# Another order of DVE and ACT instructions at the begin of nine stages of a two-block transformer kernel

## The reference, cut to what matters

```
# first block, two layers:
h = rms_norm(x, g) * (1 + sc1) + sh1 ;  x = x + g1 * mixer(h)
h = rms_norm(x, g) * (1 + sc2) + sh2 ;  x = x + g2 * conv_ffn(h)
# second block, two layers of three sublayers each:
hn = rmsnorm(x, pre_g) * (1 + scale) + shift
y  = rmsnorm(fn(hn), post_g)            # fn: swiglu, attention, swiglu
x  = x + res_w * gate * y
```

## Time and profile before

| | us |
|---|---|
| median of 3 runs | 3943.22 (3938.38 to 3943.79) |
| the profiled execution, time | 3941.97 |
| its span, first to last instruction | 3940.2 |
| PE busy | 3712.6 (94%) |
| DVE busy | 2048.6 (52%) |
| ACT busy | 1340.0 (34%) |
| mean granted TensorE clock | 0.955 |

### The profile page before, as it was taken

The page is one execution under the profiler, slowest core; times in us unless marked ns, Lnnn a source line. Parts: engine busy times, 40 slices in busy tenths (PEclk is TensorE's granted clock), DMA queues, the critical chain, the costliest instruction groups (busy, mean ns, idle before and its releaser), DMA issues.

```text
span 3940.2 us, 42183 instructions
## 1 busy us (share of the span) xinstructions
PE 3712.6 (94%) x17108; PEld 2947.2 (75%) x17108; DVE 2048.6 (52%) x3576; ACT 1340.0 (34%) x2299; POOL 127.9 (3%) x126
## 2 busy tenths in 40 slices
PE   6899999999999999979989998999899999989998
PEld 4647888757888788856678887888677777767886
DVE  7856656776766655457653345334433333354233
ACT  3553323453323322334432232223222322233222
POOL 3330000000000000001100000000000000000000
PEclk9999999989999999989989998999899999979999
DMA  6214554414555454210122222222211121112221
GB/s 243 94 44 170 203 192 177 149 34 147 199 192 197 169 196 176 86 67 23 38 75 97 96 97 70 96 96 99 71 58 59 58 67 59 54 43 81 96 97 64
DMA packets 125023, 426.58 MB, mean 108 GB/s; under 512 B 16107, under 2 KB 21099, under 8 KB 124828
## 3 DMA queue, kind: packets, MB, share of 16 engines
q1 hardware_dynamic: 124828, 423.88, 30.8%
HBM read 421.68 MB, written 2.14 MB: 108 GB/s over the span
## 4 chain that ended last, share of the span: by engine, by line
PE 84%; DVE 11%; ACT 3%; issue 1%; POOL 0%; ACTq 0%; DVEq 0%; POOLq 0%
PE ps L409 24%; PE ps L410 24%; PE ps L411 24%; PE ps L708 1%; DVE X L1597 1%; PE ps L446 1%; PE ps L755 1%; PE ps L748 1%; DVE mrow L2051 1%; DVE TT L1516 1%; PE ps L798 1%; PE ps L787 1%; DVE HL L1505 1%; PE ps L554 1%; PE ps L453 1%
## 5 line engine op out<-in xcount | busy, mean ns | idle before, releaser
L409 PE MATMUL ps<-HH,whi 128*128 128x512 f32 x3168 | 1279.2, 404 | 71.9 <-DVE HL L1505 38.9
L410 PE MATMUL ps<-HL,whi 128*128 128x512 f32 x3168 | 1258.4, 397 | 0.0
L411 PE MATMUL ps<-HH,wlo 128*128 128x512 f32 x3168 | 1256.1, 397 | 0.0
L1453 DVE TENSOR_TENSOR wlo<-wraw,whi 128x1024 fp32r<-128x1024 f32 x526 | 643.2, 1225 | 721.8 <-ACT whi L920 721.6
L920 ACT ACTIVATE whi<-wraw 128x1024 fp32r<-128x1024 f32 x548 | 575.2, 1054 | 701.4 <-PE ps L411 694.1
L409 PEld LDWEIGHTS ps<-HH,whi 128*128 128x128 f32 x3168 | 610.8, 193 | 235.5 <-issue 77.6
L410 PEld LDWEIGHTS ps<-HL,whi 128*128 128x128 f32 x3168 | 611.8, 193 | 130.8 <-issue 4.8
L411 PEld LDWEIGHTS ps<-HH,wlo 128*128 128x128 f32 x3168 | 610.1, 193 | 131.4
L1441 DVE CUSTOM_DVE_ANT_0 mraw<-mraw,CB 128x1024 f32<-128x1024 f32 x224 | 283.0, 1264 | 1.5 <-DMA mraw<-mst 1.3
L1632 DVE TENSOR_TENSOR TT<-TT,ps 128x512 f32<-128x512 f32 x116 | 79.7, 687 | 223.1 <-PE ps L411 192.4
L409 PE MATMUL ps<-PHf,whi 128*128 128x512 f32 x352 | 136.9, 389 | 0.0
(11 more groups left out here) (329 smaller groups left out, 4044.1 us busy)
## 6 DMA issues: line engine op xcount, KB each, us to landing
wraw<-wst SPq DMA_DIRECT2D x548, 512.0 KB, 3.4
mraw<-mst SPq DMA_DIRECT2D x224, 512.0 KB, 3.5
MR<-mst SPq DMA_DIRECT2D x16, 512.0 KB, 14.2
X<-xt SPq DMA_DIRECT2D x8, 256.0 KB, 5.5
BB<-bvec SPq DMA_DIRECT2D x8, 256.0 KB, 3.7
out<-X SPq DMA_DIRECT2D x8, 256.0 KB, 2.0
CB<-crow SPq DMA_DIRECT2D x2, 512.0 KB, 4.5
BB<-bvec SPq DMA_DIRECT2D x8, 128.0 KB, 3.5
```

What stands on the lines that cost most here:

```text
L409: e.matmul(o[key], wh, sh(k), start=k == 0, stop=False)
L410: e.matmul(o[key], wh, sl(k), start=False, stop=False)
L411: ins = e.matmul(o[key], wl, sh(k), start=False, stop=k == nk - 1)
L1453: e.tensor_tensor(wlo[:, x % SPLIT, :], wraw[:, x % RAW, :], whi[:, x % SPLIT, :].bitcast(F32), ALU.subtract).then_inc(*wlo_made.up(x))
```

## The change

In `modulate` of DVE, begins E to I update one tile ahead instead of two, and low(m) comes in the same turn as b(m): update(0), b(0), update(1), low(0), b(1), update(2), low(1), and so on. The wait for the root p stands just ahead of b(0), behind update(0). In all nine begins DVE and ACT do a `feed(8)` in the turns m = 1, 4 and 6, for one block each; in E to I that is behind low(m), in A to D behind low(m-1). The first feed of each stage is shorter by these 24 tiles. Nothing is computed otherwise. The diff, with context cut:

```
@@ ACT modulate
                     e.activation(HH[:, m, :], T[m % 5], ACT.Identity, bias=MOD[:, v, m:m + 1]).then_inc(
                         *a_norm.up(("hh", s, m)))
+                    if m in (1, 4, 6):
+                        feed(8)
@@ ACT and DVE, ffn, odd and dilated (each of the six places)
-                        feed(32)
+                        feed(8)
@@ ACT and DVE, mla
-                feed(48)
+                feed(24)
@@ DVE modulate
                 lane.wait_ge(v_mod, ("mod", v))
-                lane.wait_ge(mm_done, ("root", s))
+                if after is None:
+                    lane.wait_ge(mm_done, ("root", s))
                 for m in range(8):
                     if m >= 5:
                         lane.wait_ge(v_norm, ("hl", s, m - 5))
                     if after is not None:
+                        if m == 0:
+                            update(0)
                         lane.wait_ge(v_norm, ("x", after, m))
+                        lane.wait_ge(mm_done, ("root", s))
                     e.scalar_tensor_tensor(T[m % 5], X[:, m, :], AM[:, idx, m:m + 1], R, ALU.mult, ALU.mult).then_inc(
                         *v_norm.up(("b", s, m)))
-                    if m < 6 and update is not None:
-                        update(m + 2)
-                    if m:
+                    if after is not None:
+                        if m < 7:
+                            update(m + 1)
+                        low(m)
+                    elif m:
                         low(m - 1)
-                low(7)
+                    if m in (1, 4, 6):
+                        feed(8)
+                if after is None:
+                    low(7)
@@ DVE post_norm
                 else:
-                    update(0)
-                    update(1)
                     modulate(z, v, nxt, s, update)
```

## The result

| | before | changed |
|---|---|---|
| median, first comparison (4 runs each) | 3940.8 us | 3897.29 us (3894.24 to 3900.61) |
| ratio to before, 95% interval | | 0.9901 (0.9889 to 0.9912) |
| the profiled execution, time and span | 3941.97, 3940.2 | 3898.84, 3897.1 |
| mean granted TensorE clock | 0.955 | 0.962 |

The changed kernel is 1.0% faster. Two further comparisons of it gave 0.9913 (0.9899 to 0.9926) and 0.9898 (0.9882 to 0.9914), medians 3900.7 and 3895.9; the mean of the three ratios is 38 us of gain. The forecast was 3908, a gain of 35.

What follows compares the result with a forecast made beforehand. PE bounds the kernel, on the last-ending chain for 84% of the span, so only its waits or low clock yield time. Gains of 38.0 less 2.8 give 35.2 us: forecast 3908 us, range 3899 to 3926 (own range 3899 to 3917).

Steps and rivals of the forecast that it cites:

- The earlier start: Begins E to I: PE's first feature matmul starts 2.77 us earlier; bounds 2.2 and 3.3.
- The second stop: E to I: PE's stop for B2's wlo goes; with starts, gains 26.7 (F, G, I), 6.4 (H), 4.9 us (E).
- neither engine hides a gain of the other: F's first group: DVE's chain ends at 2027.16 and PE's own at 2027.13, so both give the same.
- A to D: Begins A to D: feeds between low(m) delay HL, a loss of 2.8 us, bounds 0 and 4 x 6.
- The mechanism of turn 6: A to D: ACT's B4 split starts late, so PE waits 0.4 to 0.6 us for HL(6) in all four.
- The waits of turn 1: A to D: HL(1) comes late after feature tile 0; PE waits 0, 0.5, 0, 0.3 us.
- The sum: All nine begins: 38.0 us gained less 2.8 lost, 35.2 us; profiled execution 3906.8.
- Rival 1: E to I: splits between low(m) only move the stop, only the earlier start counts; 3932 us, chance 0.11.
- Rival 2: All begins: the clock falls in PE's short waits; 3938 us in all nine, 3923 in half; chance 0.11.
- Rival 3: A to D: DVE, ACT and PE wait on one another, 14.3 us a begin lost; 3961 us, chance 0.05.
- Rival 4: B2 is early, but another wait ends at the same instant; 3942 us, chance 0.03.
- SP's loads only move ahead: SP's queue keeps its order, loading when an older wlo is made, so loads only get earlier; no size given.

Runs made afterwards that it cites:

- yn_two: Changed kernel without feeds in A to D, yn(1) ahead of b(0) and feeds in turns 1 and 4 only in E to I; 3891.51 us, 0.9884.
- yn_first: Changed kernel without feeds in the turns of A to D, and with yn(1) ahead of b(0) in E to I; 3895.09 us, ratio 0.9891.
- feeds_only: Kernel before the change, plus feeds in turns 1, 4 and 6 of E to I alone, old order kept; 3910.72 us, ratio 0.9937.
- feeds_in_b: Changed kernel without feeds in the turns of A, C and D, those of B and E to I kept; 3898.23 us, ratio 0.9905.

## Why the prediction was right, step by step

- **The earlier start** was 2.77 us a begin; measured 2.68 (6.80 to 4.12 from the last spread matmul, in all five). The wait for the root p, which no row before showed, is there with 0.66; my times gave 0.54 (1999.54 less about 1999.0), so it was sized 0.1 too small; without it I would have given 3.3 a begin.
- **The second stop** gone: 26.7 for F, G, I, 6.4 for H and 4.9 for E, with the starts; measured 26.7, 6.3 and 5.2. Of F's 6.23 beyond the start, 3.4 are the stop and the rest is the second low-clock stretch. That the two engines end together in F shows too: HL(7) is written at 2023.69, and PE starts tile 7 at 2023.75, 0.16 us later than its own pace of 2.72 a tile gives. I had written that so neither engine hides a gain of the other; the repeats show that one can: in the second profile of the changed kernel the clock rose earlier in F, tile 1 began 4.42 us after the first matmul instead of 5.23, and tile 7 still began 21.75 behind it (21.74 in the first profile), since HL comes no sooner:

```profile
2006.89 0.47 PE L409 MATMUL ps<-HH,whi 128*128 128x512 f32 x1 [3.06 <-DVE HL L1507]
...
2022.59 0.50 PE L409 MATMUL ps<-HH,whi 128*128 128x512 f32 x1 [0.21 <-DVE HL L1507]
...
2028.64 0.50 PE L409 MATMUL ps<-HH,whi 128*128 128x512 f32 x1 [0.24 <-DVE HL L1507]
```

  So here DVE's chain sets the end, and an earlier rise of the clock gains nothing. Where a feed fewer stands in the chain it does: G's group lasts 24.05 in yn_two with such a rise.
- **A to D** was 2.8; 3.1 over all profiles, and 3.7 in the first pair. The mechanism of turn 6 is in A's row, where PE idles 0.23 ahead of tile 6; from start to start the tile comes 0.4 late in A, C and D and 0.6 in B, as forecast:

```profile
369.37 0.47 PE L409 MATMUL ps<-HH,whi 128*128 128x512 f32 x1 [0.23 <-DVE HL L1507]
```

  That is 1.8 of the 3.1. The waits of turn 1, 0.5 in B and 0.3 in D, never came: tile 0 took 5.2 to 5.3 us there in every profile with feeds, and HL(1) was in time. What fills the sum is the longer low clock in D, which I had not priced. So its size is right in part by luck. In the first pair B's loss of 1.9 is of that kind too: 26.82 was the one short B of nine without feeds, 28.0 to 28.3 in the others.
- **The sum** was 35.2 for the begins; 34.5 in the first pair of profiles and 33.6 in the second. The profiled execution took 3898.84 where the sum gave 3906.8: 7.9 lower, which is the 8.6 of the untouched stretches less 0.7 in the begins. The mla and dilated stretches vary without any edit to them: the one came back to 268.95 in the changed kernel, and the other was 735.92 and 732.76 in two executions of yn_two and 739.78 in yn_first. And the median lay 1.6 under that execution, where I had added 1.25. The first median lies 1.7 us under the low end of my range, the other two on either side of it. So the mechanism in E to I held and the number was 11 us too high; what fell short is the width: I took bounds for waits and none for the clock of untouched stretches, where three profiles of one kernel span 3890.7 to 3902.9.
- **Rival 1** (the stop only moved) is refuted by feeds_only: the groups last 24.1 to 24.6. **Rival 2**: in begins F to I the clock is low once each and 1.00 behind it. The Trainium skill's rule on micro-idles ("TensorE: Matmul & The Clock Gate", "A second HAM failure mode: psum-queue depth-cycling") does not bite here: in the changed kernel's three profiles PE idled up to 0.3 us before tiles 5 and 7 in F to I and 0.2 to 0.4 before tile 6 in A to D, and no low stretch followed in the group. **Rival 3**: A to D lose 0.8 us a begin, not 14. **Rival 4**: no other wait took the place of the two; the begins of E to I are shorter by 38.3.
- **One claim was wrong without a price.** I wrote that SP's loads only move ahead. In E, ACT's split of B4 waited for a load, and with it HL(7) came at 1724.90, 4.5 us later than DVE's chain gives:

```profile
1720.38 1.06 ACT L920 ACTIVATE whi<-wraw 128x1024 fp32r<-128x1024 f32 x1 [4.64 <-DMA wraw<-wst]
```

SP's queue holds a DMA of the rotary table there that waits for all eight x, and B4's load stands behind it. PE wants tile 7 of E only at 1729.71, so there it cost nothing. B4's own `wlo` is nearer: where the clock rose earlier PE waited for it in E by 0.4 us (feeds_in_b), 0.5 (yn_first) and 0.6 (yn_two), each time behind a split that had waited for its load. With 4 columns, where PE wants tile 7 about 22 us after its start, it would have been late by about 4 us; that wasn't tried.

## What to carry to other kernels

Where a producer feeds a consumer from two chains (here HL and the weight blocks), starting one earlier gains nothing, and can lose (here 0.2%), until the other's late member is made between the first ones; write both chains out against the consumer's own pace before choosing the order. Leave the interleaving out where the consumer has no stop, since each piece between still delays the chain. Judge a change of 1% by the stretches that it touches: here the rest differed between profiles by up to a third of the gain.

## What I had not expected of the hardware

The same instructions took 262.3, 264.1 and 269.0 us in three executions of one kernel, at a mean granted clock of 0.97, 0.96 and 0.94, and the windowed attention 194.3 to 201.0 over all kernels with its instructions unchanged. These stretches have short matmuls and many waits. In the windowed attention the clock fell for 17 to 34 us in one piece (once for two pieces of 10), and how long differed between executions; what decides it I could not settle. In the first groups of F to I of the changed kernel, by contrast, the time repeats within 0.1 us though the clock rises up to 0.8 us earlier in some, since there HL sets the end. In the kernel before it does not: I's group took 30.84 and 29.49 in its two profiles.
